# A fused decoder layer on one core: the prologue before the first projections is rebuilt around x^T and a feature-outer first tile

## What is computed

```python
c_act = silu(c)
mod = c_act @ w_ada + b_ada                      # 6 x 1024: sh1, sc1, gt1, sh2, sc2, gt2
h = rmsnorm(x, norm1_g) * (1.0 + sc1) + sh1
qkv, z, b_lg, a_lg, s_b, s_c, s_x, g_a, g_b = split_cols(h @ w_in)
y_b = (s_b * causal_depthwise_conv(s_c * s_x, conv_sc_w)) @ w_proj_b
# beta and the log decay of the delta rule come from b_lg and a_lg (8 heads each)
```

## Time and profile before

| what | value |
|---|---|
| median of 3 runs | 2247.26 us (2243.89 to 2248.32) |
| the profiled execution's own time | 2244.73 us |
| its span in the trace | 2243.0 us |
| PE busy | 2055.8 us (92%) |
| DVE busy | 1369.1 us (61%) |
| ACT busy | 977.5 us (44%) |
| HBM read / written | 337.49 MB / 48.82 MB |

### The profile page before, as it was taken

How to read it: one execution, slowest core, us unless ns; L and a number is a source line. 1 busy time by engine, 2 the same in 40 slices (tenths; PEclk the granted TensorE clock), 3 DMA queues, 4 the chain that set the end, 5 groups by cost and what they waited for, 6 DMA issues and landing times.

```text
span 2243.0 us, 29727 instructions
## 1 busy us (share of the span) xinstructions
PE 2055.8 (92%) x10079; PEld 1696.2 (76%) x10079; DVE 1369.1 (61%) x2065; ACT 977.5 (44%) x1312; POOL 150.7 (7%) x106
## 2 busy tenths in 40 slices
PE   2599999999999999999999999996499999999995
PEld 2287878788787888878888787775388888888872
DVE  6535344211557475574755725434699999999985
ACT  2311111222425336253362524222278888888863
POOL 0000000000000000000000000000012222222210
PEclk9999999999999999999999999997699999999997
DMA  5233332122212021120211157734299999999965
GB/s 195 72 121 99 98 122 76 57 69 72 68 34 73 28 63 49 33 71 28 64 49 33 54 188 253 228 108 164 89 368 379 382 383 383 384 379 388 397 260 231
DMA packets 211356, 369.55 MB, mean 165 GB/s; under 512 B 42949, under 2 KB 155382, under 8 KB 185718
## 3 DMA queue, kind: packets, MB, share of 16 engines
q1 hardware_dynamic: 193542, 321.82, 41.0%
q10 hardware_dynamic: 8416, 30.44, 3.7%
q0 software_dynamic: 9360, 16.80, 2.0%
HBM read 337.49 MB, written 48.82 MB: 172 GB/s over the span
## 4 chain that ended last, share of the span: by engine, by line
PE 82%; DVE 10%; ACT 2%; issue 2%; DMA 1%; SPq 1%; DVEq 0%; ACTq 0%; POOLq 0%
PE ps L625 37%; PE ps L2282 16%; PE ps L2320 8%; PE ps L2220 4%; DVE ada_b L1289 2%; PE ps L2095 2%; PE ps L2127 2%; PE ps L2123 1%; PE ps L2268 1%; PE ps L2036 1%; DVE h_tmp L1330 1%; DMA ada_b<-in_w_ada_dram 1%; PE ps L2234 1%; PE ps L2163 1%; PE ps L2134 1%
## 5 line engine op out<-in xcount | busy, mean ns | idle before, releaser
L625 PE MATMUL ps<-h_hi,w_lo 128*128 128x512 f32 x1152 | 470.0, 408 | 2.4 <-DVE prod L1383 1.2
L530 DVE TENSOR_TENSOR mw_lo<-mw_raw,mw_hi 128x2048 fp32r<-128x2048 f32 x192 | 436.8, 2290 | 45.9 <-ACT mw_hi L525 45.9
L625 PE MATMUL ps<-h_hi,w_hi 128*128 128x512 f32 x1152 | 453.1, 393 | 0.0
L625 PE MATMUL ps<-h_lo,w_hi 128*128 128x512 f32 x1152 | 452.5, 393 | 0.0
L525 ACT ACTIVATE mw_hi<-mw_raw 128x2048 fp32r<-128x2048 f32 x192 | 368.2, 1919 | 111.7 <-PE ps L2282 65.3
L625 PEld LDWEIGHTS ps<-h_hi,w_lo 128*128 128x128 f32 x1152 | 219.2, 190 | 45.8 <-issue 3.7
L625 PEld LDWEIGHTS ps<-h_hi,w_hi 128*128 128x128 f32 x1152 | 218.5, 190 | 46.8
L625 PEld LDWEIGHTS ps<-h_lo,w_hi 128*128 128x128 f32 x1152 | 219.4, 190 | 41.6 <-issue 1.9
L590 DVE TENSOR_TENSOR w_lo<-w_raw,w_hi 128x1024 fp32r<-128x1024 f32 x88 | 107.5, 1223 | 205.7 <-ACT w_hi L585 203.9
L2282 PE MATMUL ps<-mw_hi,xT_lo 128*128 128x512 f32 x512 | 203.9, 398 | 6.8 <-DVE mw_lo L530 5.2
L2282 PE MATMUL ps<-mw_hi,xT_hi 128*128 128x512 f32 x512 | 201.1, 393 | 0.0
(11 more groups left out here) (362 smaller groups left out, 3297.4 us busy)
## 6 DMA issues: line engine op xcount, KB each, us to landing
mw_raw<-in_w_dram SPq DMA_DIRECT2D x192, 1024.0 KB, 7.9
w_raw<-in_w_in_dram SPq DMA_DIRECT2D x72, 512.0 KB, 4.0
ada_b<-in_w_ada_dram SPq DMA_DIRECT2D x9, 2048.0 KB, 8.1
y_t<-y_d SPq DMA_DIRECT2D x8, 1024.0 KB, 10.0
ada<-in_w_ada_dram SPq DMA_DIRECT2D x2, 2048.0 KB, 11.4
x_t<-in_x_dram SPq DMA_DIRECT2D x8, 512.0 KB, 3.3
w_raw<-in_w_proj_b_dram SPq DMA_DIRECT2D x8, 512.0 KB, 3.7
merged_b_d<-sc_y ACTq DMA_DIRECT2D x8, 512.0 KB, 2.6
```

The lines of the kernel that those rows point to most:

```text
L530: dve.tensor_tensor(mw_lo[off % NSPLIT][:], mw_raw[off % NRAW][:], mw_hi[off % NSPLIT][:], ALU.subtract).then_inc(mw_lo_done, 1)
L625: last = pe.matmul(dst, lhs[:, s, k], rhs[:, k, cols], start=(k == 0 and part == 0), stop=(k == KD - 1 and part == 2))
```

## The change

Loads: x comes first (`load_x`, four buffers), then the three weight tiles of conv iteration 0, then shift and scale columns of `w_ada` as sixteen pieces of 128 features x 1024 columns (512 KB; `ada_sh` and `ada_sc` in turn), with at most three pieces under way and x tiles 4 to 7 between them.

Work: normalized x is turned and copied to `x_rows` without scale and shift (half a tile by ACT, half by DVE). The shift is still summed on DVE, piece by piece between x tiles (`shift_piece`), with one PE sum at the end. The scale is computed on PE (`scale_piece`: eight matmuls for each of eight pieces, weights are the piece, the moving operand is a column of `c_act`) and summed by a DVE reduce. Then scale and shift are applied on whole feature rows of 1024 tokens (`h_make`), ACT and DVE split them, and PE takes conv iteration 0 with the feature block as outer loop over all six banks. The gate logits' halves, transposes and sums stand behind iteration 0 and inside iterations 1 and 2. The matmuls of the projections are the same in number and shape; the chunk sum of `ada_b` in iterations 0 to 7 is the same too.

```diff
+            def load_x(n):
+
+                if n >= 2:
+                    sp.wait_ge(x_in[n % 2], 16 * (n // 2))
+                if n >= 4:
+                    sp.wait_ge(x_normed, n - 3)
+                sp.dma_start(x_t[:, n % 4], x_d[n * P:(n + 1) * P, :]).then_inc(x_in[n % 2], 16)
+
+            CONV_COLS = (SC0 + D, SC0 + 2 * D, SC0)
             for n in range(4):
-                if n == 3:
-                    for t in range(2):
-                        sp.dma_start(x_t[:, t], x_d[t * P:(t + 1) * P, :]).then_inc(x_in[t], 16)
-
-                    sp.wait_ge(ada_step, 1)
-                sp.dma_start(ada_chunks[n], w_ada_d[:, :, n * 4 * P:(n + 1) * 4 * P]).then_inc(ada_in[n % 3], 16)
-            with sp.Fori(1, TT // 2) as i:
-                for s in range(2):
-
-                    row = sp.snap((2 * i + s) * P)
-                    sp.wait_ge(x_normed, 2 * i + s - 1)
-                    sp.dma_start(x_t[:, s], x_d[bass.ds(row, P), :]).then_inc(x_in[s], 16)
-
-            with sp.Fori(0, KD) as i:
-                for p, col in enumerate((SC0 + D, SC0 + 2 * D, SC0)):
+                load_x(n)
+            for p, col in enumerate(CONV_COLS):
+                load_w(sp, "conv", 0, p, w_in_d, col)
+            for n in range(2 * KD):
+                k, dst = n // 2, (ada_sh, ada_sc)[n % 2]
+                if n >= 3:
+                    sp.wait_ge(ada_in[n % 3], 16 * (n // 3))
+                sp.dma_start(dst[:, k], w_ada_d[:, k, (n % 2) * D:(n % 2 + 1) * D]).then_inc(ada_in[n % 3], 16)
+                if n in (1, 3, 5, 7):
+                    load_x(4 + n // 2)
...
+            sp.wait_ge(x_normed, TT)
+            sp.wait_ge(ada_in[2], 16 * 5)
+            load_ada(0)
...
+            def turned_x(n):
+                act.wait_ge(x_turned, past(2 * n + 1))
+                act.activation(x_rows[:, 0:4, n * P:(n + 1) * P], ps[:, 2 * (n % 2)].rearrange("p (k t) -> p k t", t=P),
+                               ACT.Copy).then_inc(x_copied, 1)
+
+            for n in range(TT):
+                act.wait_ge(x_in[n % 2], 16 * (n // 2) + 16)
+                if n:
+                    act.wait_ge(x_squared, n)
+                act.activation(x_sq[:], x_t[:, n % 4], ACT.Square, accum_out=ssq[:, 0, n:n + 1]).then_inc(x_squared, 1)
+                if n:
+                    turned_x(n - 1)
+                act.wait_ge(x_mean, n + 1)
+                act.activation(ssq[:, 1, n:n + 1], ssq[:, 2, n:n + 1], ACT.Sqrt).then_inc(x_root, 1)
+                if 4 <= n < 7:
+                    split_w_hi(act, "conv", 0, n - 4)
+            turned_x(TT - 1)
+            for k in range(KD):
+                act.wait_ge(h_summed, k + 1)
+                act.activation(h_hi[:, k], h_sum[:, k], ACT.Copy).then_inc(h_hi_done, 1)
...
+            conv_act(0)
+            gate_row_half(0)
+            conv_act(1)
...
+            def shift_piece(k):
+                dve.wait_ge(ada_in[2 * k % 3], 16 * (2 * k // 3 + 1))
+                ada_add(ada_sh, 0, k)
+
+            def turned_x(n):
+                dve.wait_ge(x_turned, past(2 * n + 2))
+                dve.tensor_copy(x_rows[:, 4:8, n * P:(n + 1) * P], ps[:, 2 * (n % 2) + 1]
+                                .rearrange("p (k t) -> p k t", t=P)).then_inc(x_copied, 1)
+
+            dve.memset(prod[:, 0:SC_TAPS - 1], 0.0)
             dve.wait_ge(cols_ready, 3)
-            for n in range(4):
-                dve.wait_ge(ada_in[n % 3], 16 * (n // 3 + 1))
-                ada_sum(ada_chunks[n], n)
+            dve.wait_ge(gate_w_split, 1)
+            dve.tensor_tensor(w_gate_lo[:], w_gate[:], w_gate_hi[:], ALU.subtract).then_inc(gate_w_split, 1)
+            for n in range(TT):
+                col = slice(n, n + 1)
+                dve.wait_ge(x_squared, n + 1)
+                dve.tensor_scalar(ssq[:, 2, col], ssq[:, 0, col], 1.0 / D, EPS, ALU.mult, ALU.add).then_inc(x_mean, 1)
+                if n:
+                    turned_x(n - 1)
+                dve.wait_ge(x_root, n + 1)
+                dve.reciprocal(ssq[:, 2, col], ssq[:, 1, col]).then_inc(conv_step, 1)
+
+                dve.wait_ge(conv_step, n + 1)
+                if n >= 2:
+                    dve.wait_ge(x_turned, past(2 * n - 2))
+                dve.tensor_scalar(x_n[:, n % 2], x_t[:, n % 4], ssq[:, 2, col], None, ALU.mult).then_inc(x_normed, 1)
+                if n >= 4:
+                    shift_piece(n - 4)
+                if 5 <= n < 8:
+                    split_w_lo(dve, "conv", 0, n - 5)
+            turned_x(TT - 1)
+            for k in range(4, KD):
+                shift_piece(k)
...
+            dve.tensor_reduce(mod[:, 1], ps[:, 6, 0:KD * KD].rearrange("p (k m) -> p m k", m=KD), AX.X, ALU.add)\
                .then_inc(mod_ready, 1)
...
+            def h_make(k):
+                dve.tensor_scalar(h_sum[:, k], x_rows[:, k], scale1[:, k:k + 1], mod[:, 0, k:k + 1], ALU.mult, ALU.add)\
+                   .then_inc(h_summed, 1)
+
+            h_make(0)
+            for k in range(KD):
+                if k + 1 < KD:
+                    h_make(k + 1)
+                dve.wait_ge(h_hi_done, past(k + 1))
+                dve.tensor_tensor(h_lo[:, k], h_sum[:, k], h_hi[:, k], ALU.subtract).then_inc(h_lo_done, 1)
...
+            def scale_piece(k):
+                pe.wait_ge(ada_in[(2 * k + 1) % 3], 16 * ((2 * k + 1) // 3 + 1))
+                for m in range(KD):
+                    last = pe.matmul(ps[:, 6, k * KD + m:k * KD + m + 1], ada_sc[:, k, m * P:(m + 1) * P],
+                                     c_act[:, k:k + 1], start=True, stop=True)
+                return last
+
+            for n in range(TT):
+                pe.wait_ge(x_normed, n + 1)
+                if n >= 2:
+                    pe.wait_ge(x_copied, 2 * (n - 1))
+                for k in range(KD):
+                    last = pe.transpose(ps[:, 2 * (n % 2) + k // 4, (k % 4) * P:(k % 4 + 1) * P],
+                                        x_n[:, n % 2, k * P:(k + 1) * P], ident[:])
+                    if k % 4 == 3:
+                        last.then_inc(x_turned, 1)
+                if n >= 4:
+                    scale_piece(n - 4)
+            for k in range(4, KD):
+                last = scale_piece(k)
+            last.then_inc(ada_used, 1)
+            ada_chunk(ada_sh, 0, KD, 0)
...
+            for p in range(3):
+                wait_w(pe, "conv", 0, p)
+            pe.wait_ge(x_copied, 2 * TT)
+            for k in range(KD):
+                pe.wait_ge(h_lo_done, past(k + 1))
+                for p in range(3):
+                    for n in range(2):
+                        last = project(pe, ps[:, 2 * p + n], "conv", p, h_hi, h_lo, n, ks=range(k, k + 1))
+                        if k == KD - 1:
+                            last.then_inc(proj_done, 1)
+            pe.wait_ge(gate_w_split, 2)
+            gate_half(0)
+            ada_chunk(ada_b, 1, 4, 4 * 4)
...
+            conv_pe(1, {0: lambda: gate_half(1), 1: gate_turn})
+            conv_pe(2, {0: gate_sums})
```

More of the change, by code:

```diff
@@ L979, in _, with conv_act @@
-            act.wait_ge(gate_logits, 4)
-            for n, kind in enumerate((G_KBG, G_KDEC, G_LAST)):
-                act.activation(gates[:, kind].rearrange("p t h -> p (t h)"),
-                               ps[:, 3, n * TT * H:(n + 1) * TT * H], ACT.Exp).then_inc(gate_exp, 1)
-            with act.Fori(0, KD) as i:
-                split_w_hi(act, "conv", i, 1)
+            def conv_act(i):
+                first = isinstance(i, int) and i == 0
+                if not first:
+                    split_w_hi(act, "conv", i, 1)
@@ L988, in _ @@
                     act.activation(sc_sb[:, n * HALF:(n + 1) * HALF], ps[:, n], ACT.Copy).then_inc(sc_copied, 1)
-                split_w_hi(act, "conv", i, 2)
+                if not first:
+                    split_w_hi(act, "conv", i, 2)
                 split_w_hi(act, *next_tile("conv", i, 2))
+                if isinstance(i, int) and i == 1:
+                    gate_row_half(1)
                 act.wait_ge(sc_y_done, past(2 * i + 2))
@@ L1950, in _, with ada_chunk @@
             pe.wait_ge(cols_ready, 3)
-            def ada_chunk(buf, chunk):
-                pe.wait_ge(ada_step, KD * chunk + KD)
-                for m in range(4):
-                    last = pe.matmul(ps[:, 7, bass.ds(chunk * 4 + m, 1)], buf[:, 0, m * P:(m + 1) * P], ones[:, 0:1],
+            def ada_chunk(buf, step, columns, first):
+                pe.wait_ge(ada_step, KD * step + KD)
+                for m in range(columns):
+                    last = pe.matmul(ps[:, 7, bass.ds(first + m, 1)], buf[:, 0, m * P:(m + 1) * P], ones[:, 0:1],
@@ L1974, in _ @@
-            pe.wait_ge(h_lo_done, past(TT))
-            pe.wait_ge(h_hi_done, past(TT))
-            pe.wait_ge(gate_w_split, 2)
-            for half in range(2):
+            def scale_piece(k):
[4 more added lines that the diff above has]
+                return last
@@ L1990, in _, with gate_turn @@
```

(31 more changed lines are left out.)

273 lines of the change are left out of this document (119 added, 154 removed).

## The result

The changed kernel takes 2215.71 us (median of 4 runs, 2214.69 to 2218.14) against 2245.57 us of the kernel before beside it (4 runs, 2243.03 to 2248.32): ratio 0.9868, 95% interval 0.9851 to 0.9885, a gain of 29.9 us. The profiled execution took 2215.41 us, its span is 2213.7 us.

The account below looks back on a forecast made before the run. PE's matmuls bound most of the span; only the 109 us before the first projection could win much. Iteration 1's equivalent start moves from 146.35 to 130.0 us, gaining 16.35: median 2247.26 - 16.3 = 2231 us, range 2217 to 2239.

Parts of the forecast that it names:

- the pace at the half level: Prologue, PE from tile 4 on: one-column matmuls run at 1.2 GHz, 0.219 us an instruction, 31.5 us for 144.
- the new wait and its length: End of conv iteration 0: PE waits 4.75 us for DVE's ada_b work, from about 114 to 119 us.
- The first rival: Prologue: the clock rises during PE's small matmuls, 13.9 us earlier, 2217 us in all; chance 0.10.
- The second rival: Prologue: small matmuls bound by their weight load, 0.328 us each, 15.7 us more, 2247 us, no change; chance 0.04.
- the third: Conv iteration 0: feature-outer block at half clock throughout, 27.6 us lost instead of 2.3, 2256 us; chance 0.04.
- The fourth: Late x tile or weight split, or second wait in iteration 1 or 2: 5 to 9 us back, 2236 to 2240; chance 0.12.
- the likeliest case: Whole kernel: gain of 16.35 us, median 2231 us, own range 2226 to 2237; chance 0.70.
- One x tile: Prologue: from one x_n's end to the next, a chain through PE and DVE of 3.93 us.
- Small matmuls at 0.219 us: Prologue, from tile 4: 64 scale and 8 shift matmuls, two instructions each, 144 instructions in 31.5 us.
- The block to the chunk: Conv iteration 0: block from 73.3 to 108.7 us, ada_b chunk closed at 119.05, iteration 1 starting at 120.95.
- `prod` to chunk, 11.72 us: End of iteration 0: DVE's taps, one w_lo and eight ada_b additions take 11.72 us from the second prod.
- Iterations 1 and 2: Conv loop: PE gains 5.6 us of gate matmuls and 1.15 of sums; transposes and gate steps stay hidden.

Follow-up runs that it names:

- e6_wide: Changed kernel with scale operands swapped: c_act column stationary, w_ada piece streamed 512 columns wide, row turned back at the end; 2208.81 us, ratio 0.9847 to the kernel before.
- r1_after: The changed kernel run again unaltered, second set, against the kernel before; 2219.15 us, ratio 0.9885.
- r3_after: The changed kernel run again unaltered, third set, against the kernel before; 2216.57 us, ratio 0.9878.
- e2_pool_scale: Changed kernel with the scale products and additions moved from PE to POOL, PE only summing at the end; 2228.47 us, ratio 0.9927 to the kernel before.

## Why the prediction was right in direction and wrong in size

Right were: the mechanism, the order of bounds, the continuous PE stream from tile 4 on, the pace at the half level, the new wait and its length, the uncovered slow start behind it, and that nothing behind the conv loop changes by design. The first rival (the clock rises during the small matmuls) is refuted: 80 instructions in 17.07 us are 0.21 each; `e6_wide` shows what that rival would have looked like (59.78, where it forecast 59). The Trainium skill (TensorE: Matmul & The Clock Gate, Part 1) has sustained busy time of PE lift the clock; for one-column matmuls the trace disagrees, with 37 us of them and of transposes without a gap, the last 20 of them alone, at 0.205 to 0.212 us an instruction. The second rival (0.328 an instruction) and the third (the block at half clock: eight slow matmuls, then full) are refuted by the same rows. The fourth is absent.

The failed step is the sum that gives 16.35 us, with its "+-3" and "the likeliest case's own range is 2226 to 2237". Its terms were mis-sized, all to the dear side, and the dips were left in it as scatter around zero.

- **One x tile**, 3.93 us: it measured 3.61 (18.40 to 22.01 and so on, 1.64 of it PE's wait). The copy took 0.69 as chosen, but the reciprocal starts 0.09 before its modelled end. From there to `x_n` it is 0.19 where 0.32 was taken, and from the start of `x_n` to PE 0.81 where 0.91 was. Tile 4 starts at 29.23 instead of 30.5: 1.3 us.
- **Small matmuls at 0.219 us** an instruction, from a row of 36 columns. A piece between two tiles took 34.27 - 30.99 = 3.28, 0.205 an instruction, the 80 in a row 0.212; 144 of them 30.3 us and not 31.5. The four transposes overlap the piece behind them and take 7.0 instead of 7.84. From tile 4 to the last shift sum it was 37.3 us, not 39.3: 2.0 us. Together, the first projection at 70.06 instead of 73.3.
- **The block to the chunk.** The block of 144 ended at 104.48: 34.4 us, not 35.4, with eight slow matmuls instead of twelve. This one is luck of the execution, as `r1_after` and `r3_after` took 35.3 and 34.8. From the block's end to the chunk it was 10.1 us in all three, not 10.35. Iteration 1 started at 116.48, not 120.95.
- **`prod` to chunk, 11.72 us**, was read from a row of the old loop. It takes 11.22 in iterations 0 to 2, which the change writes out one by one, and 11.7 again from iteration 3 on. In the loop each tap starts some 0.15 us after the step before it has ended; written out, it starts at once. The first row is the last tap of iteration 0 in the kernel before, the second the last two taps of iteration 0 after the change, without a gap between them:

```profile
136.78 1.28 DVE L1400 SCALAR_TENSOR_TENSOR sc_acc<-prod,params,sc_acc 128x1024 f32<-128x1024 f32 x1 [0.16 <-DVE sc_acc L1400]
104.91 2.60 DVE L1397 SCALAR_TENSOR_TENSOR sc_acc<-prod,params,sc_acc 128x1024 f32<-128x1024 f32 x2
```

  In iteration 0, 0.3 of these 0.5 us are lost, because the second `prod` starts 1.1 us ahead of the block's end and not 1.4.
- **Iterations 1 and 2**: 42.27 and 35.03 us, against 42.8 and 36.0. In iteration 1 PE doesn't wait for `ada_b` at all, and the chunk takes 0.79 instead of 1.05. In iteration 2 the sums took 0.61 us at full clock and not 1.15, and `prod` to chunk is again the shorter 11.22: together 1.5 us.

These are 3.2 + 1.0 + 0.3 + 1.5 = 6.0 us, a gain of 22.3 instead of 16.3; `r1_after` and `r3_after`, where the slow starts of the block and of iteration 1 took longer, give 4.6 and 4.8. Then comes the term that the sum had only as +-3: **the dips of the clock in the loop** fall from three to one, 3.3 us. That makes 25.6, which is what the two traces show at the end of the loop (398.64 - 373.03); the other pairs show 23.7 and 24.7. The rest, 4.3 us in the first set, 1.9 in the second and 2.5 in the third, lies in the 1,842 us behind the loop, where single executions of one kernel differ by up to 6.4; the changed kernel had mean clocks of 0.970 to 0.972 in the first set and 0.969 in all four runs of the second. That it is scatter of the clock is inferred, and its cause stays open. Last, the base of 2247.26 us was 1.7 to 4.4 us above the four later medians of the same kernel. So the 15.3 us between 2231 and 2215.71 are 6.0 of mis-sized terms, 3.3 of dips, 4.3 behind the loop and 1.7 of the base.

So the range failed at its low edge: 2217 came from the fast-clock rival alone, while the likeliest case, with the errors of its own terms, the dips and the base added, came to 2220, and with the scatter behind the loop to 2216.

## What to carry to other kernels

Where a prologue of narrow matmuls keeps PE busy, look at how wide they stream: the same product with operands exchanged took 1.81 us instead of 3.28 and sped up its neighbours. With the feature block as outer loop the first projection starts earlier, but all groups finish together at the end, and the engines behind PE get all their work at once. Look for what waits on that work, and move it one tile on (7.3 us here). A duration read from a loop can be longer than the same steps written out (11.72 against 11.22 us here). When small terms of a sum are each taken at their dear bound, add up their errors with one sign before you set the range.

## What the runs showed of the hardware that was not expected

- A stream of one-column float32 matmuls and transposes, 37 us without a gap and the last 20 of them one-column matmuls alone, left PE at the half level; with 512-column ones it came up within a piece (3.06, then 1.88 us).
- In `e2_pool_scale` POOL's 128x1024 float32 steps took 2.3 to 3.8 us, and DVE's `x_n` beside them up to 2.83 instead of 0.75, while copies out of PSUM stayed at 0.67 to 0.69 us.
- The dips of the clock in iterations 1 to 7 of the conv loop numbered three in each of three traces of one kernel, one in each of three traces of the other, and one or two in the variants.
- DVE's steps from `prod` to the chunk took 11.7 us inside a loop and 11.22 written out; most of the difference are gaps of some 0.15 us ahead of the taps.
